# Two-layer encoder trunk on one core: the expert layer's result is gated while it is gathered, the kept rows are fetched later, and weight halves are counted apart

## The chip, the cores and the metric

The kernel runs on one core of one Trainium2 chip. The metric is the device time of one execution in microseconds (us), as the median of several runs. Three runs of the kernel before gave 1776.89 us in the median (1775.88 to 1777.5).

## The reference

The model has two layers over 256 tokens of width 1024. Each sub-layer is x <- LayerNorm(ALPHA * x + gate(c) * f(x * (1 + scale(c)) + shift(c))), all in float32. The change touches the last sub-layer only, where f is a top-2-of-8 expert SwiGLU:

```
logits = t @ w_router + b_router
top_vals, top_idx = top_k(logits, 2)
weights = softmax(top_vals)
combine = sum(one_hot(top_idx) * weights)
out = sum over e of combine[:, e] * ((silu(t @ w_gate[e]) * (t @ w_up[e])) @ w_down[e])
x = layer_norm(ALPHA * x + gate * out, ln_w, ln_b)
```

Each of the 8 experts has an up matrix of 1024 x 7168 (gate and up side by side) and a down matrix of 3584 x 1024, so 44 MB of weights for each expert.

## The kernel before

Everything ahead of the expert layer is untouched: conditioning rows, the DeltaNet and attention mixers, a dense SwiGLU, the retention mixer and the router. It takes the first 770 us or so.

**Items.** Tokens are sorted by expert into blocks of 128 rows. One block with one expert's weights is an item. Items 0 to 7 are the eight experts, written out one after the other on every engine. An expert with more than 128 tokens gets a further item, made in a loop of three turns whose body is skipped if there is nothing to do (`over_loop`, L594); the number of further items is read from SBUF into a register. In the run shown the body is never entered.

**Units and pieces.** The weights of an item come in 21 units of 2 MB: units 0 to 13 are up columns (gate and up in turn, 512 columns each), units 14 to 20 are down rows. SyncE (SP) fetches each as two transfers of 1 MB into one of three ring slots (`expert_unit`, L670), and refills a slot when both its halves have been split (`split(sp, "w_lo", ...)`). A half is called a piece: 42 pieces for each item. For each piece ScalarE (ACT) rounds the weights to the fast matmul format into `w_hi` (`split_unit`, L1538 to L1546), VectorE (DVE) writes the rest, ring minus `w_hi`, into `w_lo` (`rest`, L1661 to L1665), and TensorE (PE) makes 12 matmuls with it: four or so products, three matmuls for each (L767 to L769: low times high, high times low, high times high). `w_hi` and `w_lo` have three buffers, so ACT may begin piece n when PE is done with piece n-3. ACT waits for both halves of the slot (`slot_landed`, L570).

**Between the matmuls.** After every second up unit ACT takes the silu (L1516), DVE multiplies with the other bank into `e_a` (L2146), PE turns the four blocks (`act_turn`, L1186 to L1190), and ACT and DVE split the turned blocks (L1564, L2153). DVE's program for an even unit u is in this order: multiply `e_a` of the pair u-2, u-1, then split unit u+1, then split the turned block. PE makes the turn right behind the first piece of unit u. After the first piece of unit 15, PE turns the rows of the next item (L1172), fetched by SP from `slots` in HBM; ACT and DVE split them.

**Results.** An item's result lies in two PSUM banks. In unit 4 of the next item ACT copies them to `ye` (`result`, L1518 to L1525) and writes `ye` to `slots`. The last item's result is not written to `slots`: it stays in PSUM and is spread over the tokens by two small matrices `hot`.

**Gathering.** GpSimd (POOL) waits until the result of item 6 is in `slots` (this is in item 7) and gathers, by four indirect transfers of 512 KB, the two rows of every token into `picked` (L2341 to L2343). ACT, in unit 12 of item 7, calls `weigh` (L1527 to L1535): it scales the residual by ALPHA, waits for the gathered rows and scales them by the router's weights, five activations in all. POOL then makes six operations of 128 x 1024 (add, gate, add; L2346 to L2350) into `hs`.

**End.** Behind item 7, in `finish`: the loop over further items is passed on every engine; DVE makes `hot` (L2165, L2167) and multiplies the last result by the gate from its banks (L2172); PE turns `hot` (L1246); ACT copies it (L1575); PE multiplies it with `ye` (L1253); DVE adds to `hs` (`add_back`, L2174 to L2179) with the moments of the layer norm between (L1700, L1702); then normalise and affine for two tiles of tokens; SP writes the output.

Of the kernel before, what the change touches and what calls it, by code (L numbers as in the profile page):

```python
# [14 lines left out]
ALU = mybir.AluOpType  # L15
# [6 lines left out]
P = 128  # L22
# [19 lines left out]
NE = 8  # L42
# [199 lines left out]
class Steps:  # L242
# [26 lines left out]
    "weighed_by weighed base_ready hot_made hot_turned hot_taken back_full first_done "  # L269
    "over_hot_made over_hot_turned over_hot_taken over_back_full over_back_free "  # L270
# [4 lines left out]
def trunk(nc, x, c, positions, cond_w, cond_b, ln_w, ln_b, ev_w_in, ev_conv_w, ev_a_log, ev_dt_bias,  # L275
# [9 lines left out]
    with ExitStack() as ctx:  # L285
# [4 lines left out]
        weights_in = [ctx.enter_context(nc.semaphore(f"weights_in{i}")) for i in range(RING)]  # L290
        bank_full = [ctx.enter_context(nc.semaphore(f"bank_full{i}")) for i in range(8)]
# [278 lines left out]
        def slot_landed(eng, it, a):  # L570
# [23 lines left out]
        def over_loop(eng, body):  # L594

            eng.wait_ge(S["over_ready"], 1)
            count = eng.value_load(over_int[0:1, 3:4], min_val=0, max_val=MAX_OVER)
# [4 lines left out]
            return count  # L602

        def finishing(eng, name, n, per, it=None):

            if it is None:
                eng.wait_ge(S[name], n)
            else:
                eng.wait_ge(S["over_" + name], it * per + (n - NE * per))

        def finished(ins, name, it=None):

            return ins.then_inc(S[name if it is None else "over_" + name], 1)
# [5 lines left out]
        def _(sp):  # L619
# [50 lines left out]
            def expert_unit(e, u, a):  # L670
# [3 lines left out]
                if u < N_UP:  # L674
                    w = moe_w_up[0, e].rearrange("(k p) n -> p k n", p=P)
                    c0 = 512 * (u // 2) + FFE * (u % 2)
                    for half in range(2):
                        sp.dma_start(to[:, half * PIECE:(half + 1) * PIECE].rearrange("p (k n) -> p k n", n=512),
                                     w[:, 4 * half:4 * half + 4, c0:c0 + 512]).then_inc(weights_in[slot], 16)
                else:  # L680
                    for half in range(2):
# [3 lines left out]
                            .then_inc(weights_in[slot], 16)  # L685
# [33 lines left out]
            over_loop(sp, over_item)  # L719
# [8 lines left out]
        def _(pe):  # L728
# [456 lines left out]
            def item(it):  # L1185
# [53 lines left out]
            for it in range(NE):  # L1239
                item(it)  # L1240

            def finish(it, over=None):

                finishing(pe, "hot_made", 1, 1, over)
                for t in range(NT):
                    last = nc.tensor.transpose(banks[HOT_BANK][:, t * P:(t + 1) * P], hot[:, 0, t], ident)  # L1246
                finished(last, "hot_turned", over)
                finishing(pe, "hot_taken", 1, 1, over)
                for h in range(2):
                    item_taken(pe, it, "down", h)  # L1250
                for t in range(NT):
                    for h in range(2):
                        finished(mm(banks[BACK_BANKS[t][h]][:], hot_T[:, t], ye[:, h], start=True, stop=True),  # L1253
                                 "back_full", over)

            def over_item(it):
                finish(it - 1, it)
                finishing(pe, "back_free", 2 * NT, 2 * NT, it)
                item(it)

            count = over_loop(pe, over_item)
            finish(count + LAST_ITEM)
# [3 lines left out]
        def _(act):  # L1266
# [236 lines left out]
            w = slot_landed(act, 0, 0)  # L1503
            for half in range(2):
                if half:
                    copy(("routerT",), logit_rows, lambda b: b[0:NE, 0:SEQ])
                f(w_hi[:, half], w[:, half * PIECE:(half + 1) * PIECE], ACT.Copy).then_inc(S["w_hi"], 1)
# [10 lines left out]
            def result(it):  # L1518

                act.wait_ge(S["slots_out"], it * 16 + 16 * FILLS)  # L1520
                for h in range(2):
                    take(it, ("down", h), ye[:, h])
# [4 lines left out]
            def weigh():  # L1527

                f(xs[:], xs[:], ACT.Copy, scale=ALPHA).then_inc(S["weighed"], 1)
# [7 lines left out]
            def item(it, first=False, earlier=None):  # L1537
                def split_unit(u):  # L1538

                    w = slot_landed(act, it, u)  # L1540
                    for half in range(2):
# [3 lines left out]
                        f(w_hi[:, n % 3], w[:, half * PIECE:(half + 1) * PIECE], ACT.Copy) \  # L1545
# [5 lines left out]
                for u in range(N_UNITS):  # L1551
                    if u == RESULT_UNIT and earlier is not None:
                        result(earlier)
                    if u == N_UP - 2 and not first and it == LAST_ITEM:
                        weigh()
# [9 lines left out]
                    if u == N_UP + 1:  # L1565
                        for half in range(2):
# [6 lines left out]
            def finish(over=None):  # L1573
                finishing(act, "hot_turned", 1, 1, over)
                finished(f(hot_T, banks[HOT_BANK][:, 0:NT * P].rearrange("p (t j) -> p t j", t=NT), ACT.Copy), "hot_taken", over)  # L1575

            def over_item(it):
                finish(it)
                item(it, first=True)

            over_loop(act, over_item)
            finish()
# [4 lines left out]
        def _(dve):  # L1587
# [544 lines left out]
            def item(it, first=False):  # L2132
# [244 lines left out]
```

## Time and profile before

| what | us |
|---|---|
| median of three runs | 1776.89 |
| the profiled execution | 1769.34 |
| its span, first to last instruction | 1767.4 |
| PE busy | 1626.9 (92%) |
| DVE busy | 1278.7 (72%) |
| ACT busy | 1015.1 (57%) |
| POOL busy | 142.2 (8%) |
| mean granted TensorE clock, as a share of full speed | 0.965 |
| moved by DMA | 515.32 MB, mean 292 GB/s |

A profile shows one execution. "Busy" of PE counts pipelined matmuls with modelled ends; how closely it works is better seen from the spacing of one matmul's start to the next. In a timeline a row with square brackets gives the engine's idle time ahead of the row and what ended it; a row without them followed its predecessor at once. A line such as L1665 is the line of the kernel printed above.

### The profile page before, as it was taken

The numbers are of one execution on the slowest core, as the hardware profiler recorded it, in microseconds if no ns is written. First come the engines' busy times: TensorE is split into PE (matmuls) and PEld (weight loads), VectorE is DVE, ScalarE is ACT, GpSimd is POOL, SyncE is SP. The second block draws the span as 40 slices with busy tenths as digits, with TensorE's granted clock in tenths as the row PEclk, the third lists the DMA queues.
The fourth block names the chain that finished last, engine by engine and source line by source line (L and its number), as shares of the span: only waits on it lengthen the run. The fifth ranks groups of instructions, "written<-read, shape, count | busy, mean of one in ns | idle before, by whom it ended". The sixth has DMA issues, their size and how long they took to land.

```text
span 1767.4 us, 19903 instructions
## 1 busy us (share of the span) xinstructions
PE 1626.9 (92%) x7810; PEld 1300.5 (74%) x7810; DVE 1278.7 (72%) x1146; ACT 1015.1 (57%) x880; POOL 142.2 (8%) x96
## 2 busy tenths in 40 slices
PE   4888996999969999789999999999999999999886
PEld 1774765878858777667888888888888888888764
DVE  1275536655465665678888889888888898888786
ACT  1432224444434544357777777777777777777663
POOL 0421310000001000220000000000000000000151
PEclk9888998999989999889999999999999999999998
DMA  9347885954445544469999999999999999999972
GB/s 330 122 165 286 311 312 188 308 189 161 153 166 175 175 143 143 167 220 387 369 385 384 369 387 383 370 384 370 381 384 369 385 383 372 386 367 385 383 278 88
DMA packets 234369, 515.32 MB, mean 292 GB/s; under 512 B 8936, under 2 KB 40960, under 8 KB 234176
## 3 DMA queue, kind: packets, MB, share of 16 engines
q1 hardware_dynamic: 228272, 491.99, 76.3%
q10 hardware_dynamic: 2992, 11.79, 1.9%
q0 software_dynamic: 3008, 10.20, 1.8%
q8 instruction: 65, 1.06, 0.2%
q14 instruction: 32, 0.26, 0.0%
HBM read 507.15 MB, written 13.11 MB: 294 GB/s over the span
## 4 chain that ended last, share of the span: by engine, by line
PE 76%; DVE 11%; DMA 7%; ACT 4%; issue 3%; SPq 0%; DVEq 0%; ACTq 0%
PE bank L767 22%; PE bank L769 22%; PE bank L768 21%; DMA ring<-in_moe_w_up 5%; DVE w_lo L1665 4%; PE bank L746 2%; ACT w_hi L1545 2%; PE bank L930 2%; DMA ring<-in_cond_w 2%; PE bank L762 1%; PE bank L1190 1%; DVE small L1700 1%; PE bank L779 0%; ACT w_part L1312 0%; DVE arena L1780 0%
## 5 line engine op out<-in xcount | busy, mean ns | idle before, releaser
L1665 DVE TENSOR_TENSOR w_lo<-ring,w_hi 128x2048 fp32r<-128x2048 f32 x336 | 770.8, 2315 | 125.4 <-ACT w_hi L1545 124.7
L1545 ACT ACTIVATE w_hi<-ring 128x2048 fp32r<-128x2048 f32 x334 | 638.8, 1917 | 211.3 <-PE bank L769 147.5
L767 PE MATMUL bank<-w_lo,heT_hi 128*128 128x512 f32 x896 | 356.5, 398 | 16.3 <-DVE w_lo L1665 14.7
L769 PE MATMUL bank<-w_hi,heT_hi 128*128 128x512 f32 x896 | 351.3, 392 | 0.0
L768 PE MATMUL bank<-w_hi,heT_lo 128*128 128x512 f32 x896 | 350.5, 391 | 0.0
L1654 DVE TENSOR_TENSOR w_part<-ring,w_part 128x1024 fp32r<-128x1024 f32 x148 | 182.9, 1242 | 224.6 <-ACT w_part L1312 223.9
L1312 ACT ACTIVATE w_part<-ring 128x1024 fp32r<-128x1024 f32 (+1 forms) x162 | 169.1, 1049 | 255.8 <-PE bank L769 250.7
L767 PEld LDWEIGHTS bank<-w_lo,heT_hi 128*128 128x128 f32 x896 | 169.3, 189 | 56.0 <-issue 22.1
L769 PEld LDWEIGHTS bank<-w_hi,heT_hi 128*128 128x128 f32 x896 | 169.0, 189 | 36.2
L768 PEld LDWEIGHTS bank<-w_hi,heT_lo 128*128 128x128 f32 x896 | 169.5, 189 | 33.7
L767 PE MATMUL bank<-w_part,hT_hi 128*128 128x512 f32 (+1 forms) x448 | 179.7, 401 | 14.4 <-DVE w_part L1654 14.4
L767 PE MATMUL bank<-w_lo,eT_hi 128*128 128x512 f32 x448 | 175.9, 393 | 0.9 <-DVE w_lo L1665 0.9
L768 PE MATMUL bank<-w_part,hT_lo 128*128 128x512 f32 (+1 forms) x448 | 175.8, 392 | 0.0
L769 PE MATMUL bank<-w_part,hT_hi 128*128 128x512 f32 (+1 forms) x448 | 175.4, 392 | 0.0
L769 PE MATMUL bank<-w_hi,eT_hi 128*128 128x512 f32 x448 | 174.6, 390 | 0.0
L768 PE MATMUL bank<-w_hi,eT_lo 128*128 128x512 f32 x448 | 174.5, 390 | 0.0
L767 PEld LDWEIGHTS bank<-w_part,hT_hi 128*128 128x128 f32 x448 | 86.1, 192 | 35.0 <-issue 11.8
L769 PEld LDWEIGHTS bank<-w_part,hT_hi 128*128 128x128 f32 x448 | 85.9, 192 | 17.8
L768 PEld LDWEIGHTS bank<-w_part,hT_lo 128*128 128x128 f32 x448 | 86.1, 192 | 17.5 <-issue 0.7
L767 PEld LDWEIGHTS bank<-w_lo,eT_hi 128*128 128x128 f32 x448 | 84.2, 188 | 18.6 <-issue 1.7
L769 PEld LDWEIGHTS bank<-w_hi,eT_hi 128*128 128x128 f32 x448 | 84.1, 188 | 17.6
L768 PEld LDWEIGHTS bank<-w_hi,eT_lo 128*128 128x128 f32 x448 | 84.2, 188 | 17.1
(346 smaller groups left out, 1593.6 us busy)
## 6 DMA issues: line engine op xcount, KB each, us to landing
ring<-in_moe_w_up SPq DMA_DIRECT2D x224, 1024.0 KB, 8.3
ring<-in_moe_w_down SPq DMA_DIRECT2D x112, 1024.0 KB, 7.0
ring<-in_cond_w SPq DMA_DIRECT2D x24, 2048.0 KB, 9.2
ring<-in_ffn_w_up SPq DMA_DIRECT2D x22, 1024.0 KB, 7.9
ring<-in_od_w_in SPq DMA_DIRECT2D x8, 2048.0 KB, 7.9
ring<-in_ev_w_in SPq DMA_DIRECT2D x5, 2048.0 KB, 12.5
ring<-in_ffn_w_down SPq DMA_DIRECT2D x5, 2048.0 KB, 7.6
ring<-in_od_w_in SPq DMA_DIRECT2D x8, 1024.0 KB, 8.0
```

The lines of the kernel that those rows point to most:

```text
L746: last = mm(bank[32 * j:32 * j + 32, :], zc[:, k, 31 - col:63 - col], w[:, k], start=(l, u) == COND_BATCHES[b][0] and k < 4, stop=False)
L762: mm(bank[:], cond_row[:, col:col + 1].broadcast_to([P, P]), acc[:, b % 2], start=True, stop=True) \
L767: mm(bank, lhs[0], rhs[1], start=start, stop=False)
L768: mm(bank, lhs[1], rhs[0], start=False, stop=False)
L769: return mm(bank, lhs[0], rhs[0], start=False, stop=stop)
L930: last = mm(bank[:, h * P:(h + 1) * P], lhs[:, n], rhs[:, n], start=True, stop=True)
L1190: last = nc.tensor.transpose(bank[:, j * P:(j + 1) * P], e_a[:, j * P:(j + 1) * P], ident)
L1312: f(part_buffer(key, 0), slot_part(act, key), ACT.Copy).then_inc(S["w_hi"], 1)
L1545: f(w_hi[:, n % 3], w[:, half * PIECE:(half + 1) * PIECE], ACT.Copy) \
L1654: tt(part_buffer(key, 1), slot_part(dve, key), part_buffer(key, 0).bitcast(F32), ALU.subtract).then_inc(S["w_lo"], 1)
L1665: tt(w_lo[:, buf], at, w_hi[:, buf].bitcast(F32), ALU.subtract).then_inc(S["w_lo"], 1)
L1700: V.do(nc.vector.bn_stats(stats[:, t, k], hs[:, t, 512 * k:512 * k + 512]))
```

## The change

- **Gate at the result's banks.** A new DVE routine `gated` multiplies the two banks by the gate on the way to `ye`, for every item, at the head of DVE's unit 4; ACT no longer copies and only starts the write to `slots`, one unit later (unit 5). POOL's gate multiplies go.
- **Gathering.** POOL also waits for the w_lo mark with which SP may fetch the last unit. ALPHA times the residual is made in two halves in units 6 and 8 of item 7; `weigh` is called behind item 7's splits and has four activations; POOL makes four additions, into `xs`.
- **hot.** DVE makes `hot` ahead of item 7; PE turns it in unit 14 of item 7, ACT copies it behind the split of unit 16, and PE waits for that copy ahead of turning the rows in unit 15. PE and DVE read the count of further items ahead of item 7.
- **Order at the end.** PE's product of `hot` with `ye` comes ahead of its loop over further items and starts as each half of `ye` is ready; in the loop the add-back now ends an item instead of opening the next.
- **Halves.** Each half of a ring slot has its own semaphore, and ACT waits for the half alone.

```diff
-            eng.wait_ge(weights_in[slot], it * (32 * SLOT_USES) + (landed[slot] + 32 * n + 32))
-            return ring[:, slot * UNIT:(slot + 1) * UNIT]
+            eng.wait_ge(half_in[slot][half], it * (16 * SLOT_USES) + (16 * n + 16))
+            return ring[:, slot * UNIT + half * PIECE:slot * UNIT + (half + 1) * PIECE]
...
             # tensor, item(it, last_one)
                             if i == 0:
                                 act_turn(N_PAIRS - 1)
+                                if last_one:
+                                    finishing(pe, "hot_made", it, 1, 1)
+                                    for t in range(NT):
+                                        last = nc.tensor.transpose(banks[HOT_BANK][:, t * P:(t + 1) * P], hot[:, 0, t], ident)
+                                    last.then_inc(S["hot_turned"], 1)
                             if i == 1:
 
                                 pe.wait_ge(S["rows_in"], it * 16 + 16)
+                                if last_one:
+                                    finishing(pe, "hot_taken", it, 1, 1)
                                 turn_tokens(lambda part: item_to_fill(pe, it, "rows_T", part))
...
+            for it in range(LAST_ITEM):
                 item(it)
+            count = over_count(pe)
+            item(LAST_ITEM, True)
+            finish(LAST_ITEM)
+            over_loop(pe, count, over_item)
...
             # scalar
             def result(it):
 
-                act.wait_ge(S["slots_out"], it * 16 + 16 * FILLS)
-                for h in range(2):
-                    take(it, ("down", h), ye[:, h])
                 for h in range(2):
                     item_taken(act, it, "down", h)
                 act.dma_start(slots[bass.ds(it * P, P)], ye[:].rearrange("p h n -> p (h n)")).then_inc(S["slots_out"], 16)
...
-                    if u == RESULT_UNIT and earlier is not None:
+                    if u == RESULT_UNIT + 1 and earlier is not None:
                         result(earlier)
-                    if u == N_UP - 2 and not first and it == LAST_ITEM:
-                        weigh()
+                    if u in (RESULT_UNIT + 2, RESULT_UNIT + 4) and not first and it == LAST_ITEM:
+                        t = (u - RESULT_UNIT - 2) // 2
+                        f(xs[:, t], xs[:, t], ACT.Copy, scale=ALPHA).then_inc(S["scaled"], 1)
...
                     if u == N_UP + 1:
+                        if last:
+                            finishing(act, "hot_turned", it, 1, 1)
+                            f(hot_T, banks[HOT_BANK][:, 0:NT * P].rearrange("p (t j) -> p t j", t=NT), ACT.Copy) \
+                                .then_inc(S["hot_taken"], 1)
...
             # vector
                 for u in range(N_UNITS):
+                    if u == RESULT_UNIT and earlier is not None:
+                        gated(earlier)
...
+            def gated(it):
+
+                dve.wait_ge(S["slots_out"], 16 * FILLS + 16 * min(it, LAST_ITEM) if isinstance(it, int) else 16 * (FILLS + LAST_ITEM))
+                for h in range(2):
+                    taken(dve, "cond", 1, 10 + h)
+                    bank, free = item_filled(dve, it, "down", h)
+                    tt(ye[:, h], bank[:], mod[:, 5 * D + 512 * h:5 * D + 512 * h + 512], ALU.mult).then_inc(free, 1)
...
+            for it in range(LAST_ITEM):
+                item(it, earlier=it - 1 if it else None)
+            make_hot(V)
+            count = over_count(dve)
+            item(LAST_ITEM, earlier=LAST_ITEM - 1)
+            over_loop(dve, count, over_item)
+            gated(count + LAST_ITEM)
...
             # gpsimd
             pool.wait_ge(S["slots_out"], 16 * (FILLS + LAST_ITEM))
+            split(pool, "w_lo", LAST_ITEM, 2 * (N_UNITS - 1 - RING) + 2)
...
-            for t in range(NT):
-                pool.wait_ge(S["weighed"], 2 + t)
-                G.then(tt(hs[:, t], hs[:, t], picked[1][:, t], ALU.add))
-                G.then(tt(hs[:, t], hs[:, t], mod[:, 5 * D:6 * D], ALU.mult))
-                tt(hs[:, t], hs[:, t], xs[:, t], ALU.add).then_inc(S["base_ready"], 1)
+            for t in range(NT):
+                pool.wait_ge(S["scaled"], t + 1)
+                pool.wait_ge(S["weighed"], t + 1)
+                G.then(tt(xs[:, t], xs[:, t], picked[0][:, t], ALU.add))
+                tt(xs[:, t], xs[:, t], picked[1][:, t], ALU.add).then_inc(S["base_ready"], 1)
```

## Rows read from the trace of the kernel before

**Rows 1.** Busy time by engine in two stretches of 100 us; PEclk, DMA share, GB/s last.

```profile
1500.00:1600.00 100.00, 99.60 (x456) 82.10 (x456) 88.38 (x52) 75.13 (x52) 0.00 (x0) 1.00 1.01 378
1600.00:1700.00 100.00, 90.31 (x391) 73.67 (x391) 79.46 (x43) 71.68 (x51) 20.30 (x9) 0.95 0.96 353
```

**Rows 2.** Chain of waits, items 5, 6, 7: PE turning the next rows (start, us, what).

```profile
1458.03 0.87 PE bank L1172 x8
...
1577.31 0.87 PE bank L1172 x8
...
1713.67 0.87 PE bank L1172 x8
```

**Rows 3.** Timeline of PE in item 7, behind its three longest stops.

```profile
1658.35 0.77 PE L767 MATMUL bank<-w_lo,heT_hi 128*128 128x512 f32 x1 [5.20 <-DVE w_lo L1665]
...
1693.11 0.77 PE L767 MATMUL bank<-w_lo,heT_hi 128*128 128x512 f32 x1 [4.49 <-DVE w_lo L1665]
1693.68 0.63 PE L768 MATMUL bank<-w_hi,heT_lo 128*128 128x512 f32 x1
...
1706.82 0.66 PE L1190 MATMUL bank<-cst,arena 128*128 128x128 f32 x4 [1.95 <-DVE arena L2146]
```

**Rows 4.** Timeline of PE at unit 4 of item 7.

```profile
1632.73 0.39 PE L769 MATMUL bank<-w_hi,heT_hi 128*128 128x512 f32 x1
1632.96 0.60 PE L1190 MATMUL bank<-cst,arena 128*128 128x128 f32 x4
```

**Rows 5.** DMA by queue, 1644 to 1652 us: packets, MB, share; then one gather's landing.

```profile
q0 software_dynamic: 484, 1.72, 55.3%
...
mod<-slots,slot_of POOLq DMA_INDIRECT x1, 9.2
```

**Rows 6.** Timeline of POOL in item 7.

```profile
1638.12 1.06 POOL L2343 DMA_INDIRECT hs<-slots,slot_of  x1 [856.00 <-DMA slots<-acc]
...
1644.56 1.01 POOL L2343 DMA_INDIRECT mod<-slots,slot_of  x1 [0.30 <-issue]
1685.99 2.40 POOL L2348 TENSOR_TENSOR hs<-hs,mod 128x1024 f32<-128x1024 f32 x1 [40.42 <-ACT mod L1534]
```

**Rows 7.** Timeline of ACT in item 7 and behind it.

```profile
1686.76 1.14 ACT L1534 ACTIVATE mod<-mod 128x1024 f32<-128x1024 f32 x1
...
1736.36 1.92 ACT L1545 ACTIVATE w_hi<-ring 128x2048 fp32r<-128x2048 f32 x1 [0.74 <-PE bank L769]
1748.27 0.39 ACT L1575 ACTIVATE mod<-bank 128x256 f32<-128x256 f32 x1 [9.99 <-PE bank L1246]
```

**Rows 8.** Timeline of DVE in items 6 and 7 and behind them.

```profile
1585.67 2.29 DVE L1665 TENSOR_TENSOR w_lo<-ring,w_hi 128x2048 fp32r<-128x2048 f32 x1 [0.37 <-ACT w_hi L1545]
...
1631.90 0.68 DVE L2146 TENSOR_TENSOR arena<-arena,bank 128x512 f32<-128x512 f32 x1
...
1689.73 7.62 DVE L1665 TENSOR_TENSOR w_lo<-ring,w_hi 128x2048 fp32r<-128x2048 f32 x2 [4.85 <-ACT w_hi L1545]
1697.28 0.68 DVE L2153 TENSOR_TENSOR eT_lo<-bank,eT_hi 128x512 fp32r<-128x512 f32 x1
...
1743.95 1.11 DVE L2165 TENSOR_SCALAR mod<-mod 128x128 f32<-128x128 f32 x4 [3.35 <-issue]
...
1745.44 1.28 DVE L2172 TENSOR_TENSOR acc<-bank,mod 128x512 f32<-128x512 f32 x2
...
1754.93 0.64 DVE L2179 TENSOR_TENSOR hs<-hs,bank 128x512 f32<-128x512 f32 x1
```

**Rows 9.** DMA issues of SP, the down units of item 7.

```profile
1678.36 46.84 SPq L683 DMA_DIRECT2D ring<-in_moe_w_down  x14
```

**Rows 10.** Waits of PE, items 1 to 6 (870 to 1577 us): total, times, longest.

```profile
PE bank L767 <- DVE w_lo L1665: 1.9, 5, 0.6
```

**Rows 11.** Waits of PE, router and item 0 (755 to 870 us).

```profile
PE bank L767 <- DVE w_lo L1665: 3.1, 4, 1.7
```

**Rows 12.** Timeline of PE behind item 7: the last product.

```profile
1748.88 5.92 PE L1253 MATMUL bank<-acc,mod 128*128 128x512 f32 x8 [0.65 <-ACT mod L1575]
```

More of the change, by code:

```diff
@@ L290, in trunk @@
         weights_in = [ctx.enter_context(nc.semaphore(f"weights_in{i}")) for i in range(RING)]
+        half_in = [[ctx.enter_context(nc.semaphore(f"half{h}_in{i}")) for h in range(2)] for i in range(RING)]
         bank_full = [ctx.enter_context(nc.semaphore(f"bank_full{i}")) for i in range(8)]
@@ L1183, in _, with item @@
                 last.then_inc(full, 1)
-            def item(it):
+            def item(it, last_one=False):
                 def act_turn(pair):
@@ L1238, in _, with finish @@
                 taken(pe, "rows_T", half)
[L1239 to L1244, printed above, removed]
-                for t in range(NT):
-                    last = nc.tensor.transpose(banks[HOT_BANK][:, t * P:(t + 1) * P], hot[:, 0, t], ident)
-                finished(last, "hot_turned", over)
-                finishing(pe, "hot_taken", 1, 1, over)
-                for h in range(2):
-                    item_taken(pe, it, "down", h)
+            def finish(it):
+                finishing(pe, "hot_taken", it, 1, 1)
                 for t in range(NT):
                     for h in range(2):
-                        finished(mm(banks[BACK_BANKS[t][h]][:], hot_T[:, t], ye[:, h], start=True, stop=True),
-                                 "back_full", over)
+                        item_taken(pe, it, "down", h)
+                        mm(banks[BACK_BANKS[t][h]][:], hot_T[:, t], ye[:, h], start=True, stop=True) \
+                            .then_inc(S["back_full"], 1)
             def over_item(it):
-                finish(it - 1, it)
-                finishing(pe, "back_free", 2 * NT, 2 * NT, it)
+                finishing(pe, "back_free", it - 1, 2 * NT, 2 * NT)
+                item(it, True)
+                finish(it)
+            for it in range(LAST_ITEM):
                 item(it)
-            count = over_loop(pe, over_item)
-            finish(count + LAST_ITEM)
+            count = over_count(pe)
+            item(LAST_ITEM, True)
+            finish(LAST_ITEM)
+            over_loop(pe, count, over_item)
         @block.scalar
@@ L1571, in _ @@
                 item(it, earlier=it - 1 if it else None)
[L1573 to L1582, printed above, removed]
+            weigh()
+            over_loop(act, over_count(act), lambda it: item(it, first=True))
             normalise(3)
@@ L2130, in _, with item @@
             nc.vector.tensor_copy(over_int[0:1, 0:3], over_id[0:1, :]).then_inc(S["over_ready"], 1)
-            def item(it, first=False):
+            def item(it, first=False, earlier=None):
                 def split_unit(u):
@@ L2156, in item, with make_hot @@
                             tokens_lo(half, item_filled(dve, it, "rows_T", half), it * 2 + (3 + half))
-            for it in range(NE):
-                item(it)
-            def finish(it, V, over=None):
+            def gated(it):
[4 more added lines that the diff above has]
+                    tt(ye[:, h], bank[:], mod[:, 5 * D + 512 * h:5 * D + 512 * h + 512], ALU.mult).then_inc(free, 1)
+            def make_hot(V):
                 for i in range(2):
@@ L2166, in finish, with add_back @@
                 V.wait()
-                finished(tt(hot[:, 0], hot[:, 0], hot[:, 1], ALU.add), "hot_made", over)
-                dve.wait_ge(S["slots_out"], 16 * (FILLS + LAST_ITEM))
-                for h in range(2):
-                    taken(dve, "cond", 1, 10 + h)
-                    bank, free = item_filled(dve, it, "down", h)
-                    tt(ye[:, h], bank[:], mod[:, 5 * D + 512 * h:5 * D + 512 * h + 512], ALU.mult).then_inc(free, 1)
-            def add_back(t, h, over=None):
+                tt(hot[:, 0], hot[:, 0], hot[:, 1], ALU.add).then_inc(S["hot_made"], 1)
+            def add_back(it, t, h, to):
                 cols = slice(512 * h, 512 * h + 512)
                 dve.wait_ge(S["base_ready"], t + 1)
-                finishing(dve, "back_full", 2 * t + h + 1, 2 * NT, over)
-                return tt(hs[:, t, cols], hs[:, t, cols], banks[BACK_BANKS[t][h]][:], ALU.add)
+                finishing(dve, "back_full", it, 2 * t + h + 1, 2 * NT)
+                return tt(to[:, t, cols], xs[:, t, cols], banks[BACK_BANKS[t][h]][:], ALU.add)
             def over_item(it):
```

56 lines of the change are left out of this document (21 added, 35 removed).

## The prediction

> **What bounds the kernel now.** I looked first at the busy times by stretch [rows 1]. In a stretch of the expert layer PE is busy 99.60 of 100 us at a granted clock of 1.00, while DMA moves 378 GB/s and DVE is busy 88: PE bounds the layer. In the stretch that holds item 7 PE drops to 90.31 and the clock to 0.95. Next the chain of waits [rows 2]: the same place of items 5 and 6 lies 119.28 us apart (1577.31 - 1458.03), that of items 6 and 7 136.36 (1713.67 - 1577.31). So item 7 loses 17.1 us. PE's timeline shows where [rows 3]: idle 5.20 us at 1658, 4.49 at 1693 and 1.95 at 1707; behind the two long ones matmuls are recorded at 0.63 us where 0.39 is usual [rows 3, 4], the mark of the half clock (1.2 GHz). Behind the third stop the clock did not fall.
>
> The first stop follows the gathers: POOL issues them from 1638.12 to 1645.6, the last lands 9.2 us behind its issue, and from 1644 to 1652 their queue takes 55.3% of the DMA time [rows 5, 6], so the weights arrive at half their pace. The second is `weigh` on ACT: the residual's two tiles and four scalings, six times a tile of 1.14 [rows 7], each overlapping the next by 0.1, so some 6 us in which no piece is rounded. The third is POOL's arithmetic beside DVE: two subtractions take 7.62 us where one took 2.29 before [rows 8].
>
> **Part 1, item 7's stops.** All three causes are moved behind the last fetch or behind the last piece. The residual's two tiles stay, near 1.0 each in units 6 and 8, where ACT waits for PE about 0.75 ahead of a piece [rows 7]: 0.3 late, covered by PE's three buffers (below). POOL now waits for the mark with which SP fetches unit 20. I take away the whole 17.1. Kept end for the range: 12, if a part comes back in the new place.
>
> **Part 2, the gathers beside the last fetch.** The last of SP's 14 issues ends at 1678.36 + 46.84 = 1725.2 [rows 9]; the gathers start then. Before, they needed 1653.8 - 1638.1 = 15.7 us from first issue to last landing [rows 5, 6], so they land by 1741, in unhurried order: the first tile's two rows by about 1735. ACT rounds its last piece from 1736.36 to 1738.3 [rows 7], so unit 20's second half has 11 us for its 2 MB, against 5.4 us alone, taking some 388 GB/s for all queues (378 over the stretch of rows 1). Even at half pace from the start it takes 10.8 us and is there at 1736.0, just in time. Cost 0; bounds 0 and 5.4 (their 2.1 MB all ahead of unit 20). The Trainium skill (DMA: Bandwidth & Descriptors, section on queues, rings and completion order) says that each DMA engine takes turns between its queues a packet at a time; the trace's 55.3% for the gathers' queue agrees. By that rule the weights lose half their pace and not their place, which is what speaks against putting gathers there at all.
>
> **Part 3, the gate on DVE.** This is a cost in each of items 1 to 7. DVE's two gate multiplies take 1.28 [rows 8] and stand ahead of `e_a` in unit 4. There `e_a` starts at 1631.90 with no idle ahead of it and ends at 1632.58; PE's turn needs it and starts at 1632.96, at once behind its predecessor [rows 4, 8]. The margin is 0.38. With 1.28 ahead, and 0.06 for the semaphore, PE stops for 1.28 - 0.38 + 0.06 = 0.96. ACT loses its two copies, but DVE is the late one here. Behind the turn the next piece is due one piece (12 x 0.23 = 2.7 us [rows 4]) later, so nothing more is lost. Seven items: **+6.7**. Bounds: 0, if DVE runs ahead; 9.0 (seven whole times 1.28).
>
> **Part 4, halves counted apart.** ACT may start a unit 2.7 us earlier (1 MB at 388 GB/s). PE waited for weights for 1.9 in items 1 to 6 [rows 10] and 3.1 in item 0 with the router, of which the longest, 1.7, is the router's work on DVE [rows 11]. So -1.9 - 1.4 = **-3.3**; bounds 0 and -5.0.
>
> **Part 5, hot.** `make_hot` ahead of item 7 is four operations in 1.11, one of 0.43 and a register read, some 2.1 on DVE. A piece is rounded in 1.92 and split in 2.29 [rows 7, 8] while PE makes two pieces in 5.5: a margin near 1.05 with two semaphores, and DVE idles 0.37 besides [rows 8]. 2.1 - 1.4 gives **+0.6** (0 to 2.1). The two turns of `hot` add 0.2. The wait for the copy of `hot` is dearer: PE reaches it right behind piece 30, when ACT, whose program has the rounding of piece 33 first, can only begin that rounding, because it waited for piece 30 too. So PE stands 1.92 + 0.39 + 0.1 [rows 7] = **+2.4**. PE's own register read is taken while matmuls are still queued: 0 (at most 1).
>
> **Part 6, the end.** Count from item 7's last matmul at 1744.5. ACT's `weigh` starts at 1738.3; its first tile is done 2.1 later, its second 4.2 later. POOL adds from 1740.4: two operations of 2.40 for each tile [rows 6], base ready at 1745.2 and 1750.0. DVE gates the last result at 1743.1 (the first bank is full six matmuls ahead of the end) and 1744.6, PE has no 3.35 of loop [rows 8] ahead of its product and, even at the recorded 5.92 [rows 12], is done by 1750.6. DVE's third add, at 1754.93 before [rows 8], then needs POOL's 1750.0: it starts at about 1750.1, and from there on the order is as before. **-4.8**. Bounds: -2.4, if POOL's additions for one tile take twice their 2.40 beside DVE, and -5.4, if the end goes by PE's product at full clock. The Trainium skill (SBUF — State Buffer, section on who interferes with whom) has POOL and DVE exclude each other where a DVE operation reads two SBUF inputs. That agrees with 7.62 for two subtractions, and with 0.68 for L2153 beside POOL, undisturbed, as one input is in PSUM [rows 8]; DVE's operations beside the new additions are of that second kind.
>
> **Sum.** -17.1 + 6.7 - 3.3 + 0.6 + 0.2 + 2.4 - 4.8 = -15.3 us. The profiled execution, 1769.3, would be 1754.0. It lies 7.6 under the median of the runs shown, which I hold to be a plain offset: 1776.9 - 15.3 = **1761.6 us**, 0.86% less.
>
> **Rivals.**
> - *DVE runs ahead.* The gate multiplies cost nothing, as ACT's relief lets the pieces come earlier. Against it: in the rows DVE reaches `e_a` with no idle time. 1761.6 - 6.7 = 1754.9. Chance 0.13.
> - *The clock falls, or the gathers crowd unit 20.* PE's new stop of 2.4 lies between 1.95 (clock kept) and 4.49 (clock fell) [rows 3]. At half clock 12 matmuls lose 0.2 each, 2.4; gathers ahead of unit 20 cost up to 5.4. 1764 to 1769. Chance 0.2. The Trainium skill (TensorE: Matmul & The Clock Gate, section on the clock gate) says an idle enough PE is put back to half its clock; by it this rival is as open as by the rows.
> - *Item 7's stops only move.* The loop of three buffers, not the gathers and `weigh`, makes them; 12 of 17.1 remain and the gate costs its 6.7: 1761.6 + 12 = 1773.6. This is also the case in which the change does not do what it says. Against: each stop has its cause in the row beside it. Chance 0.05.
> - *Slower, by the chain at unit 4.* Gate multiplies hold up the split of piece 10 and with it SP's next fetch. If a late fetch made ACT and DVE miss a buffer turn, each item would lose 1.92 + 2.29 = 4.2 instead of 0.96: 7 x 3.2 = 22.7 more, 1784. It decides at a stop of PE near unit 4 above (15.3 + 6.7)/7 = 3.1 us. Against: the slot refilled by piece 9 is released ahead of the multiplies, and halves give the fetch 2.7 us. Chance 0.05.
>
> **How the numbers follow.** The forecast has 0.57. A measurement of this kernel tells 0.2%, some 3.6 us, from no change. Forecast, first and second rival are faster; the third lies on the edge and is counted as no change, with 0.01 for a weaker form of the fourth. Faster 0.89, same 0.06, slower 0.05. The range takes the first rival, with 2 for unsure terms, at its lower end (1753) and the second at its upper (1769).
>
> **What would show it.** In the profile after: PE's idle ahead of matmuls in item 7 without the 5.20 and 4.49; a wait of PE for DVE's `e_a` near 1.0 in unit 4 of items 1 to 7, and so an item of about 119.9 us; a wait of PE near 2.4 for `hot_T` ahead of the turn of L1172 in item 7, with the clock kept; DVE's third add ended by POOL. If PE shows no wait at unit 4, part 3 is wrong; if ACT waits for DMA at unit 20, part 2; if PE still waits 5 us in the middle of item 7, part 1.

## The result, and the profile after

| us | before | changed |
|---|---|---|
| median of the runs | 1776.39 (1774.51 to 1777.5, 4 runs) | 1754.33 (1752.43 to 1754.79, 4 runs) |
| the profiled execution | 1769.34 | 1754.29 |
| its span | 1767.4 | 1752.5 |
| PE, DVE, ACT, POOL busy | 1626.9, 1278.7, 1015.1, 142.2 | 1618.9, 1279.0, 1009.2, 132.6 |
| mean granted clock | 0.965 | 0.966 |

The ratio of the times is 0.988, with a 95% interval of 0.9866 to 0.9894: 22 us less by the medians, 14.9 by the spans of the two profiled executions. These two numbers differ by 7, and a good part of what follows is about that.

Busy time by engine in the two stretches of [rows 1], changed kernel:

```profile
1500.00:1600.00 100.00, 99.29 (x456) 81.94 (x455) 89.75 (x54) 73.96 (x51) 0.00 (x0) 1.00 1.01 377
1600.00:1700.00 100.00, 97.98 (x445) 80.20 (x443) 89.27 (x57) 75.04 (x52) 0.00 (x0) 1.00 1.02 378
```

PE is busy 97.98 of the 100 us of item 7 where it was 90.31, at a clock of 1.00, and POOL, which was busy 20.30 there, does nothing. DMA moves 378 GB/s instead of 353. The chain of waits at the places of [rows 2] (item 6's turn of the rows is L1167 now, and item 7's):

```profile
1459.24 0.87 PE bank L1167 x8
...
1578.76 0.87 PE bank L1167 x8
...
1699.25 2.32 issue
1701.57 1.94 PE bank L1167 x8
1703.51 0.43 PE bank L762
```

An item lasts 119.52 here (1578.76 - 1459.24; before 119.28), item 7 122.81 (1701.57 - 1578.76; before 136.36). Ahead of item 7's turn stands a new 2.32 that the profile calls "issue": the wait for the copy of `hot`. The turn behind it takes 1.94 for eight where 0.87 was usual, and the next matmul 0.43: the half clock. Busy time by engine in the 4 us from the turn's start, with the granted clock behind POOL's share, says the same (0.58):

```profile
1701.57:1705.57 4.00, 4.00 (x15) 3.57 (x16) 3.25 (x3) 1.19 (x2) 0.00 (x0) 0.58 0.87 320
```

PE's waits from 870 to 1560 and from 1560 to 1760 us (total, times, longest):

```profile
PE bank L1185 <- DVE arena L2137: 4.3, 6, 0.7
...
PE bank L1167 <- issue: 2.3, 1, 2.3
PE bank L1185 <- DVE arena L2137: 0.7, 1, 0.7
PE bank L762 <- DVE w_lo L1654: 0.6, 1, 0.6
```

These four rows are all of PE's stops in items 1 to 7. The 1.9 of [rows 10] for weights and the three stops of [rows 3] are gone; in their place is one stop an item for `e_a` (L2137). PE's and DVE's timelines at unit 4 of item 7 show it, to be read beside [rows 4] and the second row of [rows 8]. PE's:

```profile
1634.99 0.39 PE L764 MATMUL bank<-w_hi,heT_hi 128*128 128x512 f32 x1
1636.09 0.66 PE L1185 MATMUL bank<-cst,arena 128*128 128x128 f32 x4 [0.72 <-DVE arena L2137]
```

DVE's:

```profile
1629.75 4.49 DVE L1654 TENSOR_TENSOR w_lo<-ring,w_hi 128x2048 fp32r<-128x2048 f32 x2 [0.85 <-ACT w_hi L1537]
1634.16 1.28 DVE L2155 TENSOR_TENSOR acc<-bank,mod 128x512 f32<-128x512 f32 x2
1635.36 0.68 DVE L2137 TENSOR_TENSOR arena<-arena,bank 128x512 f32<-128x512 f32 x1
```

The two gate multiplies (L2155) take 1.28 and stand directly ahead of `e_a`, which PE's turn waits for. The turn starts 1.10 behind its predecessor instead of 0.23: 0.87 lost. Behind the last fetch, the timeline of POOL:

```profile
1714.92 2.69 POOL L2339 DMA_INDIRECT hs<-slots,slot_of  x1 [930.43 <-DVE w_lo L1654]
...
1730.19 2.40 POOL L2343 TENSOR_TENSOR xs<-xs,hs 128x1024 f32<-128x1024 f32 x1 [4.46 <-ACT mod L1527]
...
1737.44 2.34 POOL L2344 TENSOR_TENSOR xs<-xs,mod 128x1024 f32<-128x1024 f32 x1
```

That of DVE:

```profile
1732.84 0.69 DVE L2155 TENSOR_TENSOR acc<-bank,mod 128x512 f32<-128x512 f32 x1 [2.56 <-PE bank L764]
...
1739.90 0.69 DVE L2170 TENSOR_TENSOR hs<-xs,bank 128x512 f32<-128x512 f32 x1 [1.55 <-POOL xs L2344]
```

And the DMA queues from 1715 to 1735 us (packets, MB, share of 16 engines):

```profile
q0 software_dynamic: 576, 2.10, 30.9%
q1 hardware_dynamic: 544, 2.10, 28.7%
```

The gathers start with SP's last fetch, at 1714.92. Their 2.10 MB (q0) and the 2.10 MB of unit 20 (q1) move side by side, and PE has no wait for it. The third add-back (L2170) ends its idle time on POOL's last addition (L2344), as forecast.

### The profile page after: what moved, and what is told of

It reads as the page before. It is cut to its first block, busy times and chain, and to the rows that moved or that the text cites. A ratio compares the mean times of both kernels' runs of the same rounds, so it can differ in the third digit from the quotient of the medians.

```text
span 1752.5 us, 20076 instructions
## 1 busy us (share of the span) xinstructions
PE 1618.9 (92%) x7810; PEld 1297.9 (74%) x7810; DVE 1279.0 (73%) x1160; ACT 1009.2 (58%) x867; POOL 132.6 (8%) x94
## 3 DMA queue, kind: packets, MB, share of 16 engines
q8 instruction: 65, 1.06, 0.2%
## 4 chain that ended last, share of the span: by engine, by line
PE 82%; DVE 9%; issue 3%; ACT 3%; DMA 3%; POOL 1%; SPq 0%; DVEq 0%; ACTq 0%; POOLq 0%
PE bank L762 24%; PE bank L764 23%; PE bank L763 23%; PE bank L741 2%; PE bank L925 2%; DMA ring<-in_cond_w 2%; DVE w_lo L1654 2%; PE bank L1185 1%; PE bank L757 1%; ACT w_hi L1537 1%; DMA ring<-in_moe_w_up 1%; DVE small L1689 1%; DVE acc L2155 1%; PE bank L774 0%; PE bank L1167 0%
## 5 line engine op out<-in xcount | busy, mean ns | idle before, releaser
L763 PEld LDWEIGHTS bank<-w_hi,eT_lo 128*128 128x128 f32 x448 | 84.4, 188 | 17.1
```

The costliest lines, as they stand in the source:

```text
L763: mm(bank, lhs[1], rhs[0], start=False, stop=False)
```

## The experiments

All comparisons below use one division of the span. It is cut at item 0's first matmul, then at the starts of PE's turn of the rows in the chain of waits: item 0's (turn 0), item 6's and item 7's, and then the span's end. Every entry is the difference of two such starts in that kernel's own profile. The first cut in PE's timelines, before and then changed:

```profile
769.46 0.47 PE L767 MATMUL bank<-w_lo,heT_hi 128*128 128x512 f32 x1 [1.53 <-issue]
...
771.81 0.47 PE L762 MATMUL bank<-w_lo,heT_hi 128*128 128x512 f32 x1 [1.53 <-issue]
```

| profile of | start to first matmul | from there to turn 0 | items 1 to 6 | item 7 | turn 7 to end | span |
|---|---|---|---|---|---|---|
| before | 769.46 | 92.24 | 715.61 | 136.36 | 53.7 | 1767.4 |
| changed | 771.81 | 89.98 | 716.97 | 122.81 | 50.9 | 1752.5 |
| e1 before, once more | 771.01 | 92.34 | 718.46 | 136.50 | 53.7 | 1772.0 |
| e2 gate behind the turn | 773.51 | 89.97 | 740.24 | 126.60 | 50.9 | 1781.2 |
| e3 copy of `hot` earlier | 773.08 | 89.94 | 716.98 | 120.50 | 49.3 | 1749.8 |
| e4 both halves waited for | 771.58 | 92.36 | 719.61 | 123.47 | 50.9 | 1757.9 |
| e5 changed, once more | 771.53 | 89.96 | 716.91 | 122.89 | 50.9 | 1752.2 |
| e6 before, halves apart | 772.92 | 90.19 | 711.68 | 132.90 | 52.9 | 1760.6 |
| e7 gate and write moved | 771.90 | 90.14 | 711.67 | 121.97 | 49.3 | 1745.0 |
| e8 gathers at once | 770.56 | 90.08 | 716.91 | 125.73 | 50.9 | 1754.2 |
| e9 gathers and `weigh` as before | 771.53 | 90.17 | 716.86 | 131.61 | 49.2 | 1759.4 |
| e10 e7 and e3 together | 771.03 | 90.09 | 712.26 | 119.66 | 49.2 | 1742.2 |

The first column varies by 4 us in code that no edit touches. The second falls into two groups, 92.2 to 92.4 with whole slots and 89.9 to 90.2 with halves. So the columns from the second on carry the argument. The runs against the kernel before:

| | median us (lowest to highest, runs) | before, same chip | ratio, 95% |
|---|---|---|---|
| e2 | 1778.86 (1774.0 to 1782.98, 10) | 1773.45 | 1.0031 (1.0016 to 1.0045) |
| e3 | 1750.5 (1748.59 to 1751.92, 4) | 1773.45 | 0.9869 (0.9843 to 0.9896) |
| e4 | 1757.06 (1753.95 to 1759.77, 4) | 1773.45 | 0.9904 (0.9877 to 0.993) |
| e5 | 1752.95 (1749.96 to 1754.01, 5) | 1774.88 | 0.9869 (0.9848 to 0.9891) |
| e6 | 1762.35 (1757.81 to 1766.99, 6) | 1774.88 | 0.9923 (0.99 to 0.9946) |
| e7 | 1746.84 (1743.61 to 1748.12, 5) | 1774.88 | 0.9834 (0.9811 to 0.9856) |
| e8 | 1755.85 (1755.08 to 1756.39, 4) | 1774.88 | 0.9889 (0.9864 to 0.9914) |
| e9 | 1759.7 (1758.06 to 1761.27, 4) | 1771.93 | 0.9932 (0.9917 to 0.9947) |
| e10 | 1744.02 (1740.84 to 1746.05, 5) | 1771.93 | 0.9847 (0.9831 to 0.9862) |

### e1: the kernel before, profiled once more

No edit.

> The kernel before, unchanged, to see how much one execution differs from another: the profiled one lay 7.1 us under the median of the timed ones, while the changed kernel's lay on its median. If that was a plain offset of one execution (my prediction's view), this profile shows item 7 at 136.4 us again (turn of the rows to turn of the rows) and the end as before. Rival: item 7's stops differ from execution to execution, and this one shows them longer by up to 7 us.

It took 1773.89. The chain of waits, at the turns of items 2, 3 and 4:

```profile
1101.70 0.87 PE bank L1172 x8
...
1223.10 0.87 PE bank L1172 x8
...
1343.54 0.87 PE bank L1172 x8
```

PE's timeline, at its longest stop in item 3:

```profile
1167.93 0.47 PE L767 MATMUL bank<-w_lo,heT_hi 128*128 128x512 f32 x1 [1.65 <-DVE w_lo L1665]
```

ACT's waits from 1102 to 1344 us (total, times, longest):

```profile
ACT w_hi L1545 <- DMA ring<-in_moe_w_up: 25.4, 17, 3.0
```

Items 3 and 4 last 121.40 and 120.44, 2.9 more together than in the first profile. ACT waited 17 times for weights in these two items, 25.4 in all (8 times and 11.5 in the first profile, from 1100 to 1339 us), and PE stopped where the lag was longer than its buffers cover. Item 7 and the end are the same as in the first profile to 0.2. So of the 4.6 that this execution takes beyond the first, 1.55 lie ahead of the expert layer and 2.85 in items 1 to 6. I read the 2.85 as late weights; PE's own waits for weights there rose by 2.0 of it (1.9 to 3.9). The first profiled execution of before was one with few late weights.

### e2: gate multiplies behind the turn's work

```diff
                 for u in range(N_UNITS):
-                    if u == RESULT_UNIT and earlier is not None:
-                        gated(earlier)
...
                         tt(eT_lo[:, to], heads(bank), eT_hi[:, to].bitcast(F32), ALU.subtract).then_inc(free, 1)
+                    if u == RESULT_UNIT and earlier is not None:
+                        gated(earlier)
```

> The changed kernel with DVE's gate multiplies behind the split of the turned block in unit 4, not ahead of e_a. Theory: PE's stop of 0.87 at unit 4 goes in each of items 1 to 7, an item falls from 119.5 to about 118.6 us, 6 us less than the changed kernel (about 1748). Rival: the stop only wanders to the next piece whose split the multiplies now delay; then items stay at 119.5 and the time at 1754.

A clear miss: slower than both kernels. The stop for `e_a` is gone and a longer one stands a few pieces later. PE's timeline at that place of item 3:

```profile
1177.30 0.77 PE L762 MATMUL bank<-w_lo,heT_hi 128*128 128x512 f32 x1 [2.83 <-DVE w_lo L1654]
1177.86 0.63 PE L763 MATMUL bank<-w_hi,heT_lo 128*128 128x512 f32 x1
```

ACT's:

```profile
1171.98 0.34 ACTq L1519 DMA_DIRECT2D slots<-acc  x1
1172.42 0.60 ACT L1513 ACTIVATE arena<-bank 128x512 f32<-128x512 f32 x1 [4.17 <-DVE acc L2155]
1172.92 5.50 ACT L1537 ACTIVATE w_hi<-ring 128x2048 fp32r<-128x2048 f32 x3
```

DVE's:

```profile
1170.62 1.28 DVE L2155 TENSOR_TENSOR acc<-bank,mod 128x512 f32<-128x512 f32 x2
1174.86 4.49 DVE L1654 TENSOR_TENSOR w_lo<-ring,w_hi 128x2048 fp32r<-128x2048 f32 x2 [2.96 <-ACT w_hi L1537]
```

ACT's program waits for the gated banks at the head of unit 5, to start the write (L1519), with the rounding of the next pieces queued behind that wait. Now that DVE multiplies only at 1170.62, ACT idles 4.17, then has three pieces to make up (5.50), and DVE and PE idle in turn. The move was right for DVE and wrong for the engine behind it. An item now takes 123.4 (740.24 / 6), 4.8 more than in e7 below, which has the same gate and no such wait. The stop is 3.0 of it, from one matmul's start to the next (1174.08 to 1177.30, less the usual 0.23). Most of the rest is the half clock behind it: the next nine matmuls take 3.67 instead of 2.05, at a granted clock of 0.50 from 1177.3 to 1179.3 and 0.62 from there to 1181.

### e3: the copy of `hot` one place earlier on ACT

```diff
+                    if u == N_UP + 1 and last:
+                        finishing(act, "hot_turned", it, 1, 1)
+                        f(hot_T, banks[HOT_BANK][:, 0:NT * P].rearrange("p (t j) -> p t j", t=NT), ACT.Copy) \
+                            .then_inc(S["hot_taken"], 1)
                     if u < N_UNITS - last:
...
                     if u == N_UP + 1:
-                        if last:
...
```

> The changed kernel with ACT's copy of hot_T ahead of the rounding of unit 16 instead of behind it. Theory: PE's stop of 2.5 ahead of the turn of the rows goes, and with it the half clock behind it (1.8), 4.3 less in all (about 1750). Rival: the copy then delays the rounding and PE stops 0.4 at the next piece; or the clock falls all the same, and only 2.5 go (1752).

ACT's timeline in item 7:

```profile
1696.25 0.58 ACT L1561 ACTIVATE eT_hi<-bank 128x512 fp32r<-128x512 f32 x1
1696.72 0.38 ACT L1555 ACTIVATE mod<-bank 128x256 f32<-128x256 f32 x1
1697.82 1.92 ACT L1537 ACTIVATE w_hi<-ring 128x2048 fp32r<-128x2048 f32 x1 [0.72 <-PE bank L764]
```

The copy (L1555 here) falls into a gap in which ACT waits for PE anyway. Item 7 is shorter by 2.31 (122.81 to 120.50), the end by 1.6 (50.9 to 49.3), and the turn takes its 0.87 again. So by the profiles the wait cost 2.3, and 1.6 more because of the half clock behind it. The medians are too coarse for this: the changed kernel was not timed on this chip, and the ratios to before overlap (0.9869 here, 0.988 and 0.9869 for the changed kernel).

ACT comes to unit 20's last piece earlier than in the changed kernel and finds it not quite landed:

```profile
1723.37 1.92 ACT L1537 ACTIVATE w_hi<-ring 128x2048 fp32r<-128x2048 f32 x1 [0.94 <-DMA ring<-in_moe_w_down]
```

Its idle time there is 0.80 for the pieces ahead, so it is 0.14 late, and PE does not stop.

### e4: the changed kernel, waiting for both halves

```diff
-            eng.wait_ge(half_in[slot][half], it * (16 * SLOT_USES) + (16 * n + 16))
+            for h in range(2):
+                eng.wait_ge(half_in[slot][h], it * (16 * SLOT_USES) + (16 * n + 16))
```

> The changed kernel with ACT waiting for both halves of a slot again. Theory: PE waits for weights again, 1.9 to 3.9 in items 1 to 6 and 1.4 to 2.3 in item 0, 3.3 to 6.2 more than the changed kernel in all (1758 to 1760), and besides, unit 20 comes late behind the gathers by up to 2.7. Rival: the halves gave nothing once unit 4 has its stop, which gives the fetches time: items 1 to 6 as in the changed kernel, only item 0 longer (1756 or less).

ACT's waits for DMA while up units come, 870 to 1580 us:

```profile
ACT w_hi L1538 <- DMA ring<-in_moe_w_up: 31.4, 24, 3.7
```

PE's for weights:

```profile
PE bank L763 <- DVE w_lo L1655: 1.5, 2, 1.3
```

The changed kernel has neither row. Waiting for both halves brings back 2.4 in item 0, 2.6 in items 1 to 6 and 0.7 in item 7; ACT waits 24 times for up weights, but not at unit 20. The halves are thus worth 5.4 by the spans in the presence of the rest (1757.9 - 1752.5), and none of it lies at the last unit beside the gathers. This profiled execution is the slowest of e4's four, so 5.4 is one execution's figure; by the ratios to before (0.9904 against 0.988 and 0.9869) it is some 4 to 6.

### e5 and e6: the changed kernel again, and the kernel before with the halves alone

e5 has no edit. e6 takes the semaphores of the halves into the kernel before (the diff shown ahead of the prediction, its first hunk and what goes with it) and nothing else.

> The changed kernel, unchanged, timed beside the kernel before in more rounds, as the reference of this batch. The change measured -22 us and its two profiles differ by 14.9. Theory: the kernel before has stops for late weights that differ by up to 6 us from execution to execution, and the changed one has none in items 1 to 7, so its items repeat at 119.5 us and its runs lie closer together than those of before. Ratio 0.987 to 0.989.

> The kernel before with halves counted apart and nothing else. Theory: this part alone takes away PE's stops for weights in items 0 to 6 (3.3 by my prediction's rows, 9 in the second profile of before: items 3 and 4 at 121.4 and 120.4), and may soften item 7's first stop by up to 2.7: 6 to 12 less than before. Rival: it is worth only the 3.3 of the prediction and before's other variation has another cause.

e5 repeats the changed kernel's profile to 0.3 in every column. e6's chain of waits at the turns of items 6 and 7:

```profile
1574.79 0.87 PE bank L1173 x8
...
1707.69 0.87 PE bank L1173 x8
```

PE's timeline in item 7, its stops behind the gathers and the longest one:

```profile
1651.30 0.47 PE L768 MATMUL bank<-w_lo,heT_hi 128*128 128x512 f32 x1 [0.68 <-DVE w_lo L1664]
...
1656.45 0.66 PE L1191 MATMUL bank<-cst,arena 128*128 128x128 f32 x4 [2.17 <-DVE arena L2145]
...
1687.10 0.77 PE L768 MATMUL bank<-w_lo,heT_hi 128*128 128x512 f32 x1 [4.50 <-DVE w_lo L1664]
```

The same waits of ACT as above, 870 to 1580 us, are down to:

```profile
ACT w_hi L1544 <- DMA ring<-in_moe_w_up: 6.8, 7, 1.9
```

This run decides most. The halves alone take 12.5 off the median (1774.88 - 1762.35), more than the whole rest of the change does on top of them (9.4, 1762.35 - 1752.95). Items 1 to 6 have no stop of PE left: 711.68, which is 3.9 under the first profile of before and 6.8 under e1. Item 0 is 2.1 shorter. Item 7 goes from 136.4 to 132.9: the stop of 5.20 behind the gathers shrinks to 0.68 and 2.17, while the 4.49 of `weigh` stays as 4.50. The end is 0.8 shorter; 0.5 of it is PE's last product, which takes 5.39 here and 5.92 in [rows 12]. From the layer's first matmul on, this is 10.3 less than in the first profile of before and 13.3 less than in e1; the 12.5 of the medians lies between.

### e7: e2's move, and the write behind the next splits

e2's edit, and ACT's wait and write a few lines down:

```diff
-                    if u == RESULT_UNIT + 1 and earlier is not None:
-                        result(earlier)
...
                         split_unit(u + 1)
+                    if u == RESULT_UNIT + 1 and earlier is not None:
+                        result(earlier)
```

> As e2_gate_behind_turn, and ACT's wait for the gated result with the write to slots moved behind the rounding of unit 6. In e2 ACT stood in unit 5 for the gated banks, with the silu and the roundings of unit 6 behind it, and PE lost 3.0 in each item. Theory: without that wait the gate is free there: no stop at unit 4, items of 118.6 instead of 119.5, 6 less than the changed kernel. Rival: DVE has no room for 1.28 anywhere near, items stay at 119.5.

The chain of waits, at the turns of items 0 and 6:

```profile
862.04 0.87 PE bank L1167 x8
...
1573.71 0.87 PE bank L1167 x8
```

711.67 for items 1 to 6: the same as e6, which has no gate on DVE at all. So the gate multiplies cost the changed kernel 0.88 an item (5.30 over six) through their place alone, and nothing in this one. It is 6.1 faster than the changed kernel in the same series (1752.95 - 1746.84).

### e8 and e9: gathers, then `weigh` too, back in their old place

```diff
             pool.wait_ge(S["slots_out"], 16 * (FILLS + LAST_ITEM))
-            split(pool, "w_lo", LAST_ITEM, 2 * (N_UNITS - 1 - RING) + 2)
```

> The changed kernel without POOL's wait for the last fetch: the gathers start as soon as the result of item 6 is in slots, as before; weigh stays behind item 7's pieces. Theory: item 7's first stop comes back, less the 2.7 that a half counted apart gives: PE idle 2 to 3 and perhaps the half clock behind it, 2 to 5 more than the changed kernel. Rival: the gathers were harmless and weigh alone made both stops: no stop, same time.

e9 adds to this:

```diff
+                    if u == N_UP - 2 and not first and it == LAST_ITEM:
+                        weigh()
...
-            weigh()
             over_loop(act, over_count(act), lambda it: item(it, first=True))
```

> As e8_gathers_at_once (2.9 above the changed kernel), and ACT's weigh called in unit 12 of item 7 again, with its four scalings; POOL's four additions follow it there. [...] Net 3 to 6 above e8 (1758 to 1762). Rival: what the end gains outweighs it, and the place of weigh was no part of the gain (1755 or less).

PE's stops in e8 during the gathers:

```profile
1661.77 0.47 PE L762 MATMUL bank<-w_lo,heT_hi 128*128 128x512 f32 x1 [0.71 <-DVE w_lo L1654]
...
1665.83 0.50 PE L762 MATMUL bank<-w_lo,heT_hi 128*128 128x512 f32 x1 [1.09 <-DVE w_lo L1654]
```

e9's timeline of PE, at its longest stop, behind `weigh`:

```profile
1689.91 0.47 PE L762 MATMUL bank<-w_lo,heT_hi 128*128 128x512 f32 x1 [2.72 <-DVE w_lo L1655]
```

DVE's there:

```profile
1686.50 7.65 DVE L1655 TENSOR_TENSOR w_lo<-ring,w_hi 128x2048 fp32r<-128x2048 f32 x2 [3.05 <-ACT w_hi L1537]
```

POOL's:

```profile
1685.21 2.40 POOL L2344 TENSOR_TENSOR xs<-xs,mod 128x1024 f32<-128x1024 f32 x1
1687.58 4.42 POOL L2343 TENSOR_TENSOR xs<-xs,hs 128x1024 f32<-128x1024 f32 x1
```

Behind the stop of 2.72 the granted clock was 0.67 (1689.91 to 1692). Early gathers cost item 7 2.9 (125.73 - 122.81), `weigh` and POOL's additions 5.9 more (131.61 - 125.73); no run moves one of these two without the other. Part of that comes back: with the additions done early, e9's end is 1.7 shorter (50.9 to 49.2), although the clock fell behind its turn 7 as in e8 (granted clock over the next 4 us 0.61 and 0.57). So moving this work behind the last fetch gained 8.8 in the item and paid 1.7 at the end.

### e10: e7 and e3 together

> The changed kernel with both moves: the gate behind the turned block's split with the write behind the rounding of unit 6 (e7: 6.1 less), and ACT's copy of hot_T ahead of the rounding of unit 16 (e3: 3.9 less by the profiles). Theory: the two stops are apart, so the gains add up: 10 less than the changed kernel, about 1743 beside a kernel before of 1775. Rival: the second is hidden once the first is gone, 6 to 8 less.

Items 1 to 6 take 712.26, item 7 119.66, the end 49.2: shorter than the changed kernel by 4.7, 3.2 and 1.7. Beside e7 it gains 2.8 and not 4, because in e7's profile the clock did not fall behind the wait for `hot` (granted clock 1.00 over the 4 us from its turn, 0.58 in the changed kernel), so 1.6 of e3's gain was not to be had. Its median is 1744.02, against 1771.93 for before on the same chip, and its span is 10.3 under the changed kernel's. Whether it is faster than e7 as a whole is not shown: the two ran on different chips, and their ratios to before overlap (0.9847 and 0.9834). What its profile shows is item 7 without the stop of 2.3.

## Why the prediction was right, and where it was not

The forecast was faster, at 1761.6 with 1753 to 1769: the direction was right, and the median of 1754.33 lies in the range, near its lower end. For the profiled execution it said 1754.0, and 1754.29 was measured. That hit is partly luck, as the terms show.

**Part 1, item 7's stops: right.** The three stops are gone. Item 7 changed by -13.55 where the parts that fall in it (-17.1, the gate's +0.96, +0.6, +0.2, +2.4) gave -12.9. With the new costs of 4.0 (0.87, 0.6, 0.2, 2.3) added, 17.5 was taken off. e6, e8 and e9 show how it splits: the halves 3.5 (before to e6), the later gathers 2.9, the later `weigh` and additions 5.9. What is left between e6 and e9, 1.3 plus e9's own 4.0 of new costs, some 5.3, is what shortened `weigh` itself (the residual's two tiles taken out; no gate multiplies on POOL); that is a difference between two runs and was not tried alone. The gathers are shown as a cause by e8; `weigh` and POOL's additions only together, by e9. The halves cure a good part of the gathers' stop too.

**Part 2, gathers beside the last fetch: right, at 0.** The page of the Trainium skill (DMA: Bandwidth & Descriptors, section on queues, rings and completion order) has each DMA engine take turns between its queues. The trace agrees: 2.10 MB by 30.9% beside 2.10 MB by 28.7%. By it the last unit comes at half pace and not behind the gathers, and nothing waited for it, not even in e4, where ACT needs both halves. The sign that was to refute this part, ACT waiting for DMA at unit 20, did come in e3: 0.14, at no cost to PE. So the cost of 0 holds with next to no room.

**Part 3, the gate: right in its place and nearly in size.** 0.87 to 0.88 an item against 0.96; e7 takes the 5.3 of items 1 to 6 out by moving two lines. The first rival (DVE runs ahead) falls with it.

**Part 4, the halves: the step that failed.** The mechanism was right (ACT starts a unit earlier and PE's small waits go), the size was not. I counted -1.4 for item 0; it was -2.3 (92.24 to 89.98 from the layer's first matmul). I counted -1.9 for items 1 to 6, from the 1.9 of [rows 10]; it was -3.9 against that same execution (715.61 to 711.68). Part of the difference is that the idle time of a row understates what a stop costs (0.72 for 0.87 at unit 4 above); the rest was not traced. And I took the waits of one execution for those of all: in e1 the same row of waits reads 3.9 (from 870 to 1580), and items 1 to 6 took 718.46, so that the halves would take 6.8 there (e6). Alone the halves are worth 12.5, with the 3.5 of item 7 that part 1 had already counted whole; beside the rest 5.4, where the forecast had 3.3 with a bound of 5.0.

**The offset.** "Which I hold to be a plain offset" was wrong. Of e1's 4.6 above the first profile 2.85 are, by the reading above, late weights, that is, time that the change removes; so a change which removes such waits gains more on the median than on the mildest execution. Another 1.55 lie ahead of the expert layer, where the change removes nothing; of this kind 2.4 did come back, for the changed kernel's layer began that much later than in the first profile of before, and the sum for the profiled execution had no term for it. Its profiled execution, 1754.29, stands at its median. The forecast for the profiled execution held, so this step carries the whole error of 7.3 on the median (1761.6 - 1754.33).

**Part 5, hot: right, and the second rival in part.** `make_hot` cost a stop of 0.6, where 0.6 was written (2.1 - 1.4 is 0.7), and the wait for the copy 2.3 where 2.4 stood (e3). What I gave only to a rival came true too, the clock behind that wait: 1.6. Its other half, a price for gathers crowding unit 20, did not.

**Part 6, the end: right.** The third add-back waited for POOL and nothing else. The end is 2.8 shorter as it stands and 4.4 without the half clock (53.7 to 49.3 in e3), against 4.8. The Trainium skill (SBUF — State Buffer, section on who interferes with whom) has the port pair of POOL and DVE as an exclusive lock, used by DVE operations with two SBUF inputs. The traces agree both ways: POOL's additions behind item 7 take 2.34 to 2.40 beside DVE operations with an input in PSUM (0.69), while in e9, beside subtractions with both inputs in SBUF, an addition takes 4.42 and two subtractions 7.65.

**Where the sum agreed by luck.** Against the first profile of before, start to turn 0 changed by +0.1 (forecast -1.4: the layer began 2.4 later, and item 0 took 2.3 less), items 1 to 6 by +1.4 (forecast 5.8 - 1.9 = +3.9), item 7 by -13.6 (-12.9) and the end by -2.8 (-4.8): -14.9 for -15.2. Too little for the halves and a little too much for the gate stand against the clock behind the wait for `hot` and against an expert layer that began 2.4 later than in before's profile, in code that the change does not touch.

**The slower rival** did not happen. e2 shows that a loss of its size lies near, by another path: with the gate multiplies a few lines further down ACT waits for them and never for DMA (items 1 to 6), and every item loses 4.8, with the half clock in it, where the rival had 4.2 for a missed buffer turn.

**Open.** Before's own runs spread over 11 us (1768.96 to 1779.94) and the changed kernel's over 4 in the same series, but e6, with the halves and no stop in items 1 to 6, still spreads over 9. So the late weights are not the whole of before's spread, and what else is was not traced. One part is the layer's start, which varies over 4 us among the twelve profiles.

## What to carry to other kernels

Let each consumer wait for the smallest piece that has its own landing, here 1 MB and not 2: that was the edit that gained most and the one I underrated. On an in-order engine, a wait goes behind whatever others queue for; moving one operation means checking the waits for its result on the next engine too (e2 against e7: 4.8 us an item). When a sum is made on one execution, find out by its rows why it is faster or slower than the median before calling the difference an offset.

## What the hardware did that was not expected

- The same idle of 2.32 on PE ahead of turn 7 stands in seven profiles. In six of them the clock fell behind it: granted over the 4 us from the turn it was 0.58 (changed), 0.58 (e5), 0.60 (e2), 0.59 (e4), 0.57 (e8) and 0.61 (e9). In e7's it stayed at 1.00. The turn itself does not tell the two apart, for it took 1.08 in e9 and 1.06 in e7. The cost of one and the same wait was 2.3 or 3.9.
- With the halves apart the 5.20 stop behind the gathers was smaller although the gathers came at the same point of the program: stops of 0.68 and 2.17 in e6, of 0.71 and 1.09 in e8. The clock, 0.61 behind the 5.20 (1658.35 to 1662), stayed at 1.00 through e6's two (1650 to 1662).
- Among the eight profiles that run the changed kernel's own first items (changed, e2, e3, e5, e7 to e10), item 0's turn came anywhere from 860.64 to 863.48, with no edit between them ahead of it. The spread is there at the layer's first matmul (770.56 to 773.51); from it to the turn they agree to 0.3. These are up to 3 us that no step of an argument on the change can own.
